# A hybrid attention block on one core: where two pieces of work stand around a turning, in a hand-written order

## What is computed

```python
ada = c @ w_ada[l] + b_ada[l]
shift, scale, gate = jnp.split(ada, 3, axis=-1)
h = rms_norm(x, g_pre[l]) * (1.0 + scale[:, None]) + shift[:, None]
proj = h @ w_in[l]
(q_mla, c_kv, k_rope, q_diff, k_diff, v_diff,
 gate_mla, gate_diff, mg_mla, mg_diff) = jnp.split(proj, split_points, axis=-1)
```

## Time and profile before

| | us |
|---|---|
| median of three executions (764.79 to 765.27) | 764.91 |
| the profiled execution, its own time | 764.9 |
| its span in the trace | 763.1 |
| TensorE matmuls busy | 752.7 |
| TensorE weight loads busy | 625.1 |
| VectorE busy | 561.4 |
| ScalarE busy | 423.2 |

### The profile page before, as it was taken

One profiled execution on the slowest core, in us unless ns is written; L12 is line 12 of the kernel. 1 busy time (PEld: TensorE's weight loads), 2 busy tenths in 40 slices (PEclk: granted clock), 3 DMA queues, 4 the chain that ended last, 5 costly groups with the idle time before them and its releaser, 6 DMA issues.

```text
span 763.1 us, 10086 instructions
## 1 busy us (share of the span) xinstructions
PE 752.7 (99%) x3681; PEld 625.1 (82%) x3681; DVE 561.4 (74%) x824; ACT 423.2 (55%) x617; POOL 22.1 (3%) x95
## 2 busy tenths in 40 slices
PE   7999999999999999999999999999999999999997
PEld 5778888888888988888888888888888888888885
DVE  4899999888789579888987768776554556465554
ACT  5689777767657554544545564655444444444441
POOL 2000000000000000000000000011100000000001
PEclk9999999999999999999999999999999999999999
DMA  9999999999584789888887575556566666567642
GB/s 333 395 394 395 353 377 376 348 363 321 174 241 135 214 280 294 298 279 294 276 293 193 162 213 183 167 166 166 181 178 195 193 178 207 182 208 248 220 162 110
DMA packets 132556, 189.71 MB, mean 249 GB/s; under 512 B 10326, under 2 KB 68123, under 8 KB 132251
## 3 DMA queue, kind: packets, MB, share of 16 engines
q1 hardware_dynamic: 132240, 188.77, 75.7%
q10 hardware_dynamic: 266, 0.30, 0.1%
HBM read 185.90 MB, written 2.10 MB: 246 GB/s over the span
## 4 chain that ended last, share of the span: by engine, by line
PE 96%; SPq 2%; DMA 1%; ACT 0%; DVE 0%; issue 0%; DVEq 0%; ACTq 0%
PE ps L1925 17%; PE ps L1915 17%; PE ps L1927 17%; PE ps L1926 17%; PE ps L1901 8%; PE ps L1884 8%; PE ps L1887 4%; SPq L526 2%; PE ps L1720 1%; DMA w_raw<-in_w_in 1%; PE ps L1705 1%; PE ps L1735 1%; PE ps L1878 1%; PE ps L1875 1%; PE ps L1877 1%; PE ps L1694 0%
## 5 line engine op out<-in xcount | busy, mean ns | idle before, releaser
L1571 DVE TENSOR_TENSOR w_both<-w_raw,w_both 128x1024 fp32r<-128x1024 f32 x248 | 301.9, 1222 | 159.5 <-ACT w_both L1036 158.0
L1036 ACT CAST w_both<-w_raw 128x1024 fp32r<-128x1024 f32 x248 | 259.2, 1051 | 244.3 <-PE ps L1927 183.3
L1915 PE MATMUL ps<-w_both,h_both 128*128 128x512 f32 x560 | 138.5, 390 | 0.0
L1915 PEld LDWEIGHTS ps<-w_both,h_both 128*128 128x128 f32 x560 | 105.1, 188 | 22.2 <-DVE w_both L1571 0.2
L1925 PE MATMUL ps<-w_both,h_both 128*128 128x512 f32 x296 | 116.9, 395 | 0.0
L1927 PE MATMUL ps<-w_both,h_both 128*128 128x512 f32 x296 | 115.4, 390 | 0.0
L1926 PE MATMUL ps<-w_both,h_both 128*128 128x512 f32 x296 | 115.3, 389 | 0.0
L1901 PE MATMUL ps<-w_both,h_both 128*128 128x512 f32 x280 | 75.9, 393 | 0.8 <-ACT h_both L992 0.7
L1316 DVE SCALAR_TENSOR_TENSOR ada_acc<-ada_ring,cols,ada_acc 128x512 f32<-128x512 f32 x98 | 69.6, 745 | 0.5
L1925 PEld LDWEIGHTS ps<-w_both,h_both 128*128 128x128 f32 x296 | 55.6, 188 | 12.6 <-issue 1.7
L1927 PEld LDWEIGHTS ps<-w_both,h_both 128*128 128x128 f32 x296 | 55.6, 188 | 11.7
(11 more groups left out here) (267 smaller groups left out, 849.1 us busy)
## 6 DMA issues: line engine op xcount, KB each, us to landing
w_raw<-in_w_in SPq DMA_DIRECT2D x177, 512.0 KB, 4.7
ada_ring<-in_w_ada SPq DMA_DIRECT2D x128, 256.0 KB, 6.7
gate_ring<-in_w_ada SPq DMA_DIRECT2D x32, 512.0 KB, 5.5
w_raw<-in_w_out SPq DMA_DIRECT2D x32, 512.0 KB, 3.9
w_raw<-in_w_o_mla SPq DMA_DIRECT2D x16, 512.0 KB, 3.9
w_raw<-in_w_o_diff SPq DMA_DIRECT2D x16, 512.0 KB, 3.7
w_raw<-in_w_ukv SPq DMA_DIRECT2D x16, 256.0 KB, 3.3
x_tok<-in_x SPq DMA_DIRECT2D x2, 1024.0 KB, 6.2
```

The costliest lines, as they stand in the source:

```text
L1036: act.copy(w_hi[:, p % RING, :], w_raw[:, p % RING, :]).then_inc(hi_done, 1)
L1571: dve.tensor_tensor(w_lo[:, p % RING, :], w_raw[:, p % RING, :], w_hi[:, p % RING, :].bitcast(F32), ALU.subtract).then_inc(lo_done, 1)
L1915: ins = mm(ps[:, b0 + t, :], lhsT=side[:, 2 * i + r, t * P:(t + 1) * P], rhs=w[:, p % RING, r * CH:(r + 1) * CH], start=False, stop=last a ...
```

## The change

In the list of period 0 the first kept piece, which stood third, goes behind the turning, where the second one is. So the seven early visits stand in a row, the turning of group 1 comes after seven pieces and not after eight, and both kept pieces come after it.

```diff
 PERIODS = [
-    [(("vd", 0), (0,)), (("vd", 1), (0,)), 0, (("gate", 0), (0,)), (("gate", 1), (0,)),
-     (("gate", 2), (0,)), (("gate", 3), (0,)), (("q", 2), (0,)), TURN, 1],
+    [(("vd", 0), (0,)), (("vd", 1), (0,)), (("gate", 0), (0,)), (("gate", 1), (0,)),
+     (("gate", 2), (0,)), (("gate", 3), (0,)), (("q", 2), (0,)), TURN, 0, 1],
```

## The result

| | before | changed |
|---|---|---|
| median of 8 executions each, same chip, us | 764.78 (764.49 to 765.27) | 767.13 (766.56 to 767.41) |
| ratio, 95% interval | | 1.0028 [1.002, 1.0037] |
| profiled execution, its own time | 764.9 | 767.38 |
| its span in the trace | 763.1 | 765.6 |

A forecast was written before the change was run, and what follows sets the result against it. TensorE was taken as the bound, so all cost is in its waits: 1.72 + 0.34 = 2.06 us on 764.9 gives 767.0 us. The forecast's own bounds were 766.5 to 767.3, the whole range 765.9 to 768.1.

The forecast's parts named there:

- The turning, +1.72: Ahead of group 1's turning: it begins 1.00 us earlier, but TensorE has done 2.72 less by then; 1.72 us lost.
- The step's data, nothing: VectorE's last step of group 1: its two loads land by 42.56, just ahead of 42.75, so no charge.
- Two kept pieces behind the turning, nothing: Behind the turning: a second kept piece covers nothing more; the 0.46 wait moves to piece 8, no new cost.
- The low part of piece 10, +0.34: Second part of piece 10: its low part, later on VectorE, makes a wait of 0.51 from 0.17, adding 0.34 us.
- ScalarE, SyncE, and all behind piece 10, nothing: Copies and casts fit within each piece, pieces 7 to 10 land in time, later work is unaffected: no cost.
- VectorE in time: Rival at the turning: the last step ends by 42.57, the turning follows piece 6 at once; some 764.6 us, chance 0.07.
- given back: Rival behind the turning: 1.72 is lost, but other engines run ahead and later waits vanish; 765.9 us, chance 0.11.
- late data: Rival at the turning: the last step's loads land only by 43.75, the turning is no earlier; 768.0 us, chance 0.09.
- The clock falls: Rival at the turning: standing still some 1.7 us lowers TensorE's clock, one piece takes 2.72 more; 769.7 us, chance 0.03.

The follow-up runs named there:

- the experiment on the loads: Changed kernel with the two loads of group 1's last step behind piece 7 on SyncE, as before; 767.28 us, ratio 1.0027 to the kernel before.
- changed, half steps: Changed kernel with steps 6 and 7 of group 1 adding only the shift half of their rows; 765.81 us against 765.08, ratio 1.0013.
- changed, two more operations: Changed kernel with two extra VectorE operations, results unused, ahead of the last step of group 1; 767.9 us against 764.89, ratio 1.0037.
- changed, low part on GpSimd: Changed kernel with the low part of piece 6 made by GpSimd and not by VectorE; 768.15 us, ratio 1.005 to the kernel before.
- changed, three more operations: Changed kernel with three chained extra VectorE operations ahead of the last step of group 1; 768.57 us against 764.89, ratio 1.0048.

## Why the prediction was right

Predicted were 767.0 us and 2.06 us of new waits; measured are 767.13 and, by the rows, 2.02. The mechanism is confirmed term by term below. That the time itself is met within 0.13 is partly luck: the median before was 764.78 in these runs, 0.12 under the 764.9 that was added to, and 0.33 of the medians' difference is not in the rows of the change, and the two partly cancel. In the sum of the range, 764.9 + 2.3 is 767.2 and not 767.3; nothing rests on it.

- **The turning, +1.72.** Right: +1.69. Predicted was a turning 44.34 - 39.85 = 4.49 behind the start of piece 6; it came 44.79 - 40.33 = 4.46 behind it. The step followed the join at once and took its 1.54. The tie of the kernel before was real: a step made 0.60 later there lengthened the wait by 0.58. In the changed kernel a step 0.48 or 1.25 later lengthened it by 0.48 or 1.26, and a chain 1.08 shorter cut it by 1.07.
- **The step's data, nothing.** Right, and with more in hand than I saw: even from the later place on SyncE they are there in time. The rule of the Trainium skill that I set against it (DMA: Bandwidth & Descriptors, Queues, rings and completion order) changes nothing here, since the landing isn't what the step waits for.
- **Two kept pieces behind the turning, nothing.** Right: the wait of 0.46 moved to piece 8 and shrank to 0.37, worth 0.09; the next piece gave back 0.06 of that.
- **The low part of piece 10, +0.34.** Right: +0.36, with a wait of 0.55 where 0.51 was predicted. Making full and low h one piece later removes it.
- **ScalarE, SyncE, and all behind piece 10, nothing.** Right: copies in the row of visits wait 0.76 for TensorE, six visits in a row cost nothing when eight pieces stand ahead of the turning, no weight load of pieces 7 to 10 waits for a transfer, and the rest has 708.71 us on both sides.

Of the rivals, *VectorE in time* falls with the 1.99 of waiting; *given back* falls too, since the waits of 0.37, 0.55 and 0.16 are still there; *late data* falls with the experiment on the loads. *The clock falls* did not happen, but its argument was weaker than I made it. I rested it on 1.92 us of standing still at 8.70 without a fall. That row is from the opening, where one execution holds the upper level and another does not, and in the stage that counts the clock fell with 2.05 us. So the rival was put aside for a reason that doesn't hold, and that it didn't come is partly luck:

| kernel | TensorE stands still at the turning | piece 7 | pieces 6 to 10 (before: 14.54) | median less before |
|---|---|---|---|---|
| changed, half steps | 0.50 | 2.96 | 15.50 | +0.73 |
| changed (run again) | 1.57 | 2.96 | 16.56 | +1.55 |
| changed, two more operations | 2.05 | 4.43 | 17.96 | +3.01 |
| changed, low part on GpSimd | 2.38 | 5.26 | 19.85 | +3.55 |
| changed, three more operations | 2.83 | 4.41 | 18.70 | +3.68 |

The rows are of one profiled execution each; that of the fourth line was the slowest of its five, 769.94. From the second line to the third, TensorE stands still for 0.48 more and piece 7 takes 1.47 more, and pieces 8 and 10 take back 0.54, since their weight loads wait for nothing any more: 1.41 by these three, where 17.96 - 16.56 gives 1.40. In these two profiles 0.48 us more of VectorE work ahead of the turning goes with a loss of 3.42 us instead of 2.02. Of the executions without a profile only the mean clock is on record, which doesn't say where it was lower. The 2.72 that the rival charged for a piece at the lower clock was too high for the kernels with VectorE work alone, where the fall covered only part of a piece.

## What to carry to other kernels

Ahead of a point where the bounding engine waits for a chain of another one, count the cover in pieces: taking one piece of 2.72 us away costs that piece, less what the chain itself becomes earlier (here 1.00). A wait of almost nothing (0.05 lost) may be a tie and not slack; compare the end of the releaser's last instruction with the instant at which the waiting engine would have been ready. When a chain is made later, look also at what the delayed work now stands ahead of on its own queue: the smaller term, the low part of piece 10, came from there and could be removed by itself.

## What the runs showed of the hardware

- **TensorE's clock.** In this stage, standing still for 0.50 or 1.57 us left the granted clock at 1.00; with 2.05, 2.38 and 2.83 it fell to 0.50, that is 1.2 for 2.4 GHz, and the next piece took 4.41 to 5.26 instead of 2.96. The fall came as piece 7 began (2.05), while TensorE still stood (2.38) and about a microsecond behind the start of the turning (2.83), in one profile each. The Trainium skill (TensorE: Matmul & The Clock Gate, HAM oscillation — how this bites in real kernels) says that idle gaps between bursts bring the slower clock back; the three kernels agree, and the changed kernel itself shows a gap that didn't.
- **GpSimd beside VectorE.** Two operations of a step took 3.43 for 1.41 while GpSimd subtracted for 2.40 beside them. The first of the two alone took 2.77, where 0.75 is the median of that line around it; it ended at 42.12, 0.55 behind GpSimd's end (39.17 + 2.40 = 41.57), so most of its work can have been done after that. The Trainium skill (SBUF — State Buffer, SBUF: two separate sides) says that the two engines share a pair of ports that one holds for its whole instruction while the other is blocked, also where the VectorE operation has two inputs in SBUF, as here; the rows agree, with one case.
- **Narrow VectorE operations.** At 256 columns a pair took 0.87, at 512 it took 1.41: half the width is about 0.6 of the time.
